# Attention of the first block: output products by query, reciprocals applied to a bank of four steps, differential maps kept as two heads

## The reference, cut to what matters

```python
a_out = neighbourhood_attention(na_q, na_k, na_v, na_rel_bias[l])               # 4 heads of 64, with a bias
a = softmax(s1) - lam * softmax(s2)                                              # differential: two maps, one v
b_out = einsum('bhqk,bhkd->bhqd', a, v)
b_out = rms_norm(b_out, diff_subln[l]) * (1.0 - lambda_init)                     # over the 64 of a head
c_out = gqa_attention(cq, ck, gq_v)                                              # 4 heads of 64
d_out = mla_attention(q_nope, q_rope, k_nope, k_rope, mla_v)                     # 4 heads, 96 wide in q and k
mix = concatenate([a_out, b_out, c_out, d_out]) @ w_o[l]                         # 256 features of each mixer
x = x + rms_norm(mix, post_mix_norm[l])
```

## Time and profile before

| | us |
|---|---|
| median of 3 runs | 1950.72 (1950.56 to 1950.94) |
| the profiled execution | 1953.09 |
| its span in the trace | 1951.3 |
| of it, `mixA` in layer 0 | 45.75, from 88.64 to 134.39 |
| of it, `mixA` in layer 1 | 45.75, from 433.17 to 478.92 |

### The profile page before, as it was taken

One profiled execution on the slowest core, in us unless ns is written; L12 is line 12 of the kernel. 1 busy time (PEld: TensorE's weight loads), 2 busy tenths in 40 slices (PEclk: granted clock), 3 DMA queues, 4 the chain that ended last, 5 costly groups with the idle time before them and its releaser, 6 DMA issues. The chain is left out here.

```text
span 1951.3 us, 29289 instructions
## 1 busy us (share of the span) xinstructions
PE 1876.3 (96%) x11654; PEld 1638.3 (84%) x11654; DVE 1134.9 (58%) x1643; ACT 923.8 (47%) x1271; POOL 176.5 (9%) x221
## 2 busy tenths in 40 slices
PE   7999999998999999899999999999899999999998
PEld 6668999766899978689998789998679998779997
DVE  6576555767655578554545465446765445775443
ACT  4564343556434446554435455345245435564342
POOL 1400000050000030001000001002501001000000
PEclk9999999999999999799999999999999999999999
DMA  7504555550355555126555425554825454525551
GB/s 249 182 23 131 182 193 186 182 173 17 124 194 193 192 187 176 55 87 216 173 202 185 173 87 176 199 185 164 226 90 173 172 195 151 198 103 173 185 202 66
DMA packets 185357, 313.10 MB, mean 160 GB/s; under 512 B 18877, under 2 KB 67571, under 8 KB 185267
## 3 DMA queue, kind: packets, MB, share of 16 engines
q1 hardware_dynamic: 182595, 304.24, 46.0%
q0 software_dynamic: 1376, 4.38, 0.9%
q10 hardware_dynamic: 1296, 3.24, 0.5%
HBM read 309.90 MB, written 1.94 MB: 160 GB/s over the span
## 5 line engine op out<-in xcount | busy, mean ns | idle before, releaser
L1468 DVE TENSOR_TENSOR w_lo<-raw,w_hi 128x2048 fp32r<-128x2048 f32 (+2 forms) x290 | 654.5, 2287 | 287.6 <-ACT w_hi L998 286.9
L998 ACT ACTIVATE w_hi<-raw 128x2048 fp32r<-128x2048 f32 (+2 forms) x290 | 533.3, 1877 | 105.4 <-PE tr L2039 59.8
L2037 PE MATMUL acc<-w_hi,hT_hi 128*128 128x512 f32 (+2 forms) x688 | 270.0, 392 | 15.5 <-DVE w_lo L1468 8.9
L2039 PE MATMUL acc<-w_hi,hT_lo 128*128 128x512 f32 (+2 forms) x688 | 266.4, 387 | 0.0
L2038 PE MATMUL acc<-w_lo,hT_hi 128*128 128x512 f32 (+2 forms) x688 | 266.2, 387 | 0.0
L2037 PE MATMUL acc<-w_hi,aux_hi 128*128 128x512 f32 x608 | 237.1, 390 | 0.0
L2038 PE MATMUL acc<-w_lo,aux_hi 128*128 128x512 f32 x608 | 237.1, 390 | 0.0
L2039 PE MATMUL acc<-w_hi,aux_lo 128*128 128x512 f32 x608 | 236.5, 389 | 0.0
L2037 PE MATMUL up<-hT_hi,w_hi 128*128 128x256 f32 x768 | 217.7, 283 | 0.6 <-DVE w_lo L1468 0.6
L2037 PE MATMUL tr<-hT_hi,w_hi 128*128 128x256 f32 x768 | 217.3, 283 | 0.0
L2038 PE MATMUL tr<-hT_lo,w_hi 128*128 128x256 f32 x768 | 217.3, 283 | 0.0
(11 more groups left out here) (365 smaller groups left out, 2774.8 us busy)
## 6 DMA issues: line engine op xcount, KB each, us to landing
raw<-in_mlp_w_up SPq DMA_DIRECT2D x64, 1024.0 KB, 6.5
raw<-in_mlp_w_down SPq DMA_DIRECT2D x64, 1024.0 KB, 5.5
raw<-in_ffn_w_gate_up SPq DMA_DIRECT2D x88, 512.0 KB, 4.8
raw<-in_ffn_w_down SPq DMA_DIRECT2D x22, 1024.0 KB, 5.0
raw<-in_w_in SPq DMA_DIRECT2D x16, 1024.0 KB, 8.2
raw<-in_sb_w_in SPq DMA_DIRECT2D x12, 1024.0 KB, 5.2
raw<-in_moba_w_in SPq DMA_DIRECT2D x12, 1024.0 KB, 5.1
raw<-in_nsa_w_in SPq DMA_DIRECT2D x10, 1024.0 KB, 5.7
```

The source lines that it names most:

```text
L998: nc.scalar.activation(w_hi[:, p0.slot, 0:p0.floats], raw[:, p0.slot, 0:p0.floats], ACT.Copy)\
L1468: nc.vector.tensor_tensor(w_lo[:, p0.slot, 0:m], raw[:, p0.slot, 0:m], f32(w_hi[:, p0.slot, 0:m]), ALU.subtract).then_inc(sem["lo_ready"], 1)
L2037: nc.tensor.matmul(dst, hi, whi, start=first, stop=False)
L2039: return nc.tensor.matmul(dst, lo, whi, start=False, stop=last)
```

## The change

1. `STEP_ORDER` becomes 8 differential, 4 gqa, 4 NA and 4 mla steps, so that each run of four steps fills one of two banks, `acc[:, j // 4 % 2, :]`: five groups of four steps.
2. All output products have the form of the differential ones: 128x128 of `probT` stationary, 64 columns of `v` moving, queries on partitions (4 products a step, one head after the other).
3. `pair_scaled` is gone. The row sums of a group are kept (`pair_den`); `group_rec` takes the 8 reciprocals of a group at once, `group_out` takes the whole bank out of PSUM times the reciprocals. For the two differential groups the second map's reciprocals are multiplied by -lambda first, and the two halves are added after. A differential step is now transposed with both its maps.
4. ACT copies the turned probabilities of even steps, DVE those of odd ones (`by_vector`), each in full width.
5. All outputs are turned back on PE, four transposes a group (`out_turn`), in turns 15, 17, 21 and behind the last output product; the group of tiles 2 and 3 goes through a bank of `tr`, the others through the bank of `acc` that held them. `out_hi` and `out_lo` write two tiles at once.

The diff, cut to its core:

```diff
-STEP_ORDER = (4, 12, 5, 13, 6, 7, 14, 8, 9, 15, 10, 11, 0, 1, 2, 3, 16, 17, 18, 19)
+STEP_ORDER = (4, 5, 6, 7, 8, 9, 10, 11, 12, 13, 14, 15, 0, 1, 2, 3, 16, 17, 18, 19)
-            g2.order = (4, 5, 2, 3, 0, 1, 6, 7)
+            g2.order = (2, 3, 4, 5, 0, 1, 6, 7)
 # ACT
-                                         accum_out=den[:, c:c + 1]).then_inc(sem["p_exp"], 1)
+                                         accum_out=den_at(i, u)).then_inc(sem["p_exp"], 1)
...
-                    if 0 <= i - TURN_LAG < len(steps):
+                    if 0 <= j < len(steps) and not by_vector(j):
...
+                    if i == 12:
+                        act.wait_ge(sem["o_taken"], n["o_taken"] + 2)
+                        nc.scalar.activation(group_cols(4), group_cols(1), ACT.Square).then_inc(sem["diff_sq"], 1)
+                    if i == 15:
+                        out_hi(1, tr[:, (turn_index(DIFF_TURN) - 1) % 2, :], 1)
+                    if i == 17:
+                        out_hi(2, acc[:, 0, :], 2)
+                    if i == 21:
+                        out_hi(3, acc[:, 1, :], 3)
+                out_hi(4, acc[:, 0, :], 4)
 # DVE
-            def pair_scaled(step, i):
...
+                def group_rec(g):
+                    dve.wait_ge(sem["p_exp"], n["p_exp"] + 8 * (g + 1))
+                    rec = pair_rec[:, 8 * (g % 2):8 * (g % 2) + 8]
+                    link(nc.vector.reciprocal(rec, pair_den[:, 8 * (g % 2):8 * (g % 2) + 8]))
+                    if g < 2:
+                        r1 = rec.rearrange("p (t a) -> p t a", t=TT)[:, :, 2:4]
+                        link(nc.vector.tensor_scalar(r1, r1, lam[:, 4:5], None, ALU.mult))
+                def group_out(g):
+                    dve.wait_ge(sem["o_done"], n["o_done"] + 4 * (g + 1))
...
+                    ins = nc.vector.tensor_tensor(dst.rearrange("p t (a c) -> p t a c", c=HD), group_bank(g), rec, ALU.mult)
+                    if g < 2:
+                        link(ins)
+                        ins = nc.vector.tensor_tensor(group_cols(1)[:, :, 128 * g:128 * g + 128], dst[:, :, 0:128],
+                                                      dst[:, :, 128:256], ALU.add)
+                    ins.then_inc(sem["o_taken"], 1)
...
+                    if 0 <= j < len(steps) and by_vector(j):
...
+                        nc.vector.tensor_copy(probT[:, j % 2, :], tr[:, turn_index(j) % 2, :]).then_inc(sem["pt_evac_d"], 1)
+                    if i in (4, 8, 12, 16, 20):
+                        group_rec(i // 4 - 1)
+                    if i in (8, 12, 16, 20):
+                        group_out(i // 4 - 2)
+                    if i == 13:
+                        diff_root()
+                    if i == 14:
+                        diff_gain()
+                    if i == 16:
+                        out_lo(1, tr[:, (turn_index(DIFF_TURN) - 1) % 2, :], 2)
+                    if i == 18:
+                        out_lo(2, acc[:, 0, :], 4)
+                    if i == 22:
+                        out_lo(3, acc[:, 1, :], 6)
+                group_out(4)
+                out_lo(4, acc[:, 0, :], 8)
 # PE
+                def out_turn(g, bank):
+                    at = group_cols(g)
                     for k in range(2):
                         for t in range(TT):
+                            last = nc.tensor.transpose(bank[:, S * k + P * t:S * k + P * t + P], at[:, t, P * k:P * k + P], ident)
                     last.then_inc(sem["hT_tr"], 1)
...
+                    if i == 15:
+                        turn_free(turn_index(DIFF_TURN) - 1)
+                        pe.wait_ge(sem["od_ready"], n["od_ready"] + 1)
+                        out_turn(1, tr[:, (turn_index(DIFF_TURN) - 1) % 2, :])
+                    if i == 17:
+                        pe.wait_ge(sem["o_taken"], n["o_taken"] + 3)
+                        out_turn(2, acc[:, 0, :])
+                    if i == 21:
+                        pe.wait_ge(sem["o_taken"], n["o_taken"] + 4)
+                        out_turn(3, acc[:, 1, :])
...
-                                last = nc.tensor.matmul(head["out"][:, P * step["qt"]:P * step["qt"] + P], head["v"][kt],
-                                                        probT[:, j % 2, at:at + P], start=kt == 0, stop=kt == TT - 1)
+                        for u in range(2):
+                            head = step["heads"][u]
+                            at = 256 * step["qt"] + HD * head["place"]
+                            for kt in range(TT):
+                                last = nc.tensor.matmul(acc[:, j // 4 % 2, at:at + HD],
+                                                        probT[:, j % 2, P * (TT * u + kt):P * (TT * u + kt) + P],
+                                                        head["v"][kt], start=kt == 0, stop=kt == TT - 1)
                         last.then_inc(sem["o_done"], 1)
+                pe.wait_ge(sem["o_taken"], n["o_taken"] + 5)
+                out_turn(4, acc[:, 0, :])
```

## The result

The changed kernel takes 1959.36 us (median of 4 runs, 1958.00 to 1960.29), the one before 1950.64 (4 runs, 1950.56 to 1950.94): 8.7 us more, a ratio of 1.0041, 95% interval 1.0028 to 1.0053. The profiled execution of the changed kernel took 1959.32, its span is 1957.5.

The account below looks back on a forecast made before the run. PE was taken to bound the kernel. Its work of 51.5 a stage, waits of 3.4 and slow clock of 1.2 replace 45.75: +10.3 a stage, +20.6 for two, giving 1971 us, range 1966 to 1977.

Parts of the forecast that it names:

- slow clock: A 1.2 GHz stretch on PE in each stage, behind the wait for `diff_gain`: +1.2 a stage after covering 0.5 of waits.
- I take 1.03, as the start-up of a group is paid once: PE's output groups of eight instructions: 0.59 + 4 x 0.11 = 1.03 each, +8.8 a stage.
- Transposes: 20 x 0.59: PE's transposes, four in every step at 0.59 a group: 11.8 a stage, which is +1.2.
- wait (a): PE in turn 15 waits for `diff_gain` ahead of the turning back: DVE's chain 8.9 against 7.2, wait 1.7.
- (b): PE's transposes of turn 17 wait for the bank of `tr`, through ACT's and DVE's halves: 0.4.
- (c): Last group: DVE must take the bank out before PE turns it, ahead of `w_o`: a wait of 0.9.
- some tenths: Copies of turned probabilities, late in turns where DVE also takes a bank out: in all 0.4 a stage.
- both are hidden, and nothing of their gain reaches the end: DVE's 2.1 and ACT's some 2.6 in two differential turns lie behind PE's 4.5, so their savings gain nothing.
- two signs of being wrong: The prediction is wrong if PE's waits in the stage exceed 6 us, or the eight instructions start closer than 0.1.
- Cheap streaming: Rival: the second head hides, output groups of 0.59, stage 49.6, +3.8 a stage, 1958; chance 0.06.
- DVE as the bound: Rival: copies or banks out of PSUM at 1.2 or more, 3 us more a stage, 1978 to 1982; chance 0.06.
- The faster case: Rival: output products cost only their columns, stage 44.3, median 1948; chance 0.03, of this 0.02 faster.

Follow-up runs that it names:

- same-half kernel: Kernel before, output products issued head by head and both heads of a pair written to the same 64 partitions: 1954.62 us, ratio 1.0020.
- the kernel with the late turning: Changed kernel with the last turning back moved behind the first 12 matmuls of the `w_o` product: 1960.25 us, ratio 1.0051.
- the new order alone: Kernel before with only the new `STEP_ORDER` and its bookkeeping; products, scaling, copies and norm in the old form: 1959.15 us, ratio 1.0045.
- the order with one filling: Kernel before in the new order, with the output products alone done twice in each differential step: 1954.93 us, ratio 1.0024.
- with both: Kernel before in the new order, with transposes and output products done twice in each differential step: 1955.46 us, ratio 1.0030.
- DVE's savings on top: Kernel before in the new order, sums of squares one turn later, and only the ratio of the two sums applied in differential steps: 1965.76 us, ratio 1.0071.

## Why the prediction was right and wrong

**Direction, and the mechanism of the outputs: right.** PE-bound turns, eight instructions per output group that have nothing to overlap with, 0.11 from one to the next: the changed kernel shows 0.84 to 1.04 a group, and the same-half kernel measured the overlap (0.60 against 1.02).

**Size: wrong.** The forecast had 56.1 a stage, the trace has 51.35: 9.5 of the 11.6 us by which the forecast of 1971 lay too high, for two stages. Term by term, in the forecast's own terms:

| term | forecast | measured |
|---|---|---|
| scores | 12.7 | 12.5 |
| transposes | 11.8 | 10.4 |
| outputs | 20.6 | 18.7 |
| late jobs | 4.0 | 3.6 |
| turning back | 2.4 | 1.7 |
| waits | 3.4 | 4.35 |
| slow clock | 1.2 | 0 |

(The measured ones are sums over PE's starts in layer 0, from a group's start to the next one's, without the waits.)

**The step that failed** is "I take 1.03, as the start-up of a group is paid once", and with it "Transposes: 20 x 0.59". These prices were read from starts in the kernel before, and they hold two things that come less often in the changed kernel: a change of the tile's shape behind the group, and a longer start of the group. Its transposes are at 0.49, or 0.44 in mla turns, and its outputs at 0.93, or 0.84 in mla turns, with 1.03 or 1.04 in only four groups. That is 1.9 (outputs) + 1.4 (transposes) + 0.7 (turning back) = 4.0 of the 4.75 by which the stage came out shorter. The last instruction of an output group in a differential and in an mla turn:

```profile
99.76 0.28 PE L2425 MATMUL acc<-proj,probT 128*128 128x64 f32 x1
...
127.71 0.28 PE L2425 MATMUL acc<-proj,probT 128*128 128x64 f32 x1
```

The next group starts 0.20 behind the first (99.96) and 0.11 behind the second (127.82). The first is followed by scores with a stationary tile of 64*128, the second by scores of 96*128. The single starts in both stages of the changed kernel, and in the kernel before outside its slow clock, all say the same. Behind the last instruction of outputs or of transposes, the next group of the stage starts 0.11 later at the least if its tile is 128*128 or 96*128 behind one of 128*128, and 0.20 later at the least if the tile changes to or from 128*64, or from 128*128 to 32*128 or 64*128. In the changed kernel nearly all that follow no wait are at these values. The price of 0.59 for four transposes came from 131.28, ahead of products of 128*64; in the changed kernel they stand ahead of 128*128. The forecast's own rows had the smaller value beside the larger: the transposes of the late jobs at 92.89, ahead of 128*128, took 0.49 up to 93.38, and I counted 0.59 for all.

A second 0.1 is at the start of an output group. From its first instruction to its second it takes 0.06 in 14 groups of the changed stage and 0.16 in 5, of which three stand behind the waits of 0.28, 0.36 and 0.60 (131.23: 0.94 instead of 0.84). In the kernel before it is 0.16 in seven of the eight differential groups. So the 0.59 of 104.47, and with it the 1.03, held that 0.1 as well; it is why an output group in a differential turn takes 0.93. That PE pays it where it comes to its input early is my reading of the three waits, and no run was made for it.

**The clock.** "With wait (a) of the same length I expect the same stretch behind it", +1.2. Both stages of the changed kernel have a granted clock of 1.00, although the wait of 1.50 ahead of line 2375 is there. It is not that such a wait never brings a fall: the kernel with the late turning has 10.2 us of slow clock behind the same wait in one of its stages, and the one with half of the products 6.8 and 3.4. What I missed is larger than 1.2, and didn't show in the total: the new order alone has 17 to 20 us of slow clock in a stage, most of it among the differential turns, and with the load of the new products that part is not there. The forecast had no term for the order, and that did no harm only because of the other part. The expectation for the order alone, by the same method, was 1948.5 to 1952, and the kernel took 1959.

**Waits.** (a) was 1.50 for 1.7, its chain on DVE from 109.60 to 118.22, 8.6 for 8.9. (b) was 0.82 for 0.4. (c) was 0.78 for 0.9. The forecast's "some tenths" of waits for copies were 1.24: 0.28, 0.36 and 0.60. The run with all copies on ACT says that the sharing out of the copies costs 2.3 a stage, 1.8 in waits. The forecast had two of these copies in its chain (a), at 1.3, and still wrote "both are hidden, and nothing of their gain reaches the end", from busy times alone. DVE was to be busy for well under 30 us and ACT for about 30; they are at 30.4 and 27.6. Neither of its two signs of being wrong came as it was meant: the waits are 4.35, under 6, and the eight instructions start 0.11 apart, all but the second, which mostly starts 0.06 behind the first.

**From the stage to the median.** 2 x 5.6 = 11.2 in the stages, 8.7 in the medians; the other 2.1 of the miss are here. The forecast took 2.4 off the profiled execution's time because the old one's lay so far above its median; the changed one's profiled execution lies at its median (1959.32 and 1959.36). That alone would have put the forecast 2.4 higher, so it doesn't explain the miss; it is of the size of what one execution's clock does elsewhere (the first stage began 2.4 earlier). A slip beside it: groups of 0.95 without the slow stretch give 1966, as the range has it, and not the 1967 among the rivals. Why the clock falls at other places in one execution than in another stays open, also why the order with one filling (stages of 50.4 and 51.0) has a median as low as with both (49.2 and 50.3).

**Rivals.** Cheap streaming would have given the nearest time, 1958, by groups of 0.59 that the trace doesn't have: a right number by a wrong reason. DVE as the bound is out, it is busy for 30.4 of 51.35. The faster case fell with the 0.11.

## What to carry to other kernels

A group's price from start to start depends on its neighbours. Take it from a place where the group behind it has the same tile shape as in the new kernel (0.11 or 0.20 behind the last instruction here), and where the engine comes as late to its input as it will there. If an engine of high share gets lighter work in a row, ask what its clock does: on TensorE, less work made stages longer here (51.8 with the order alone, 54.6 with DVE's savings on top), and repeating work made them shorter (49.2). And run the parts of a change apart before adding their prices: order and form cost 6.0 and 5.0 alone, and 5.6 together.

## What the hardware showed that I had not expected

- Eight instructions with 64 stationary columns each take 0.60 when the heads have different halves, whether they alternate or stand four by four, and 1.02 in the same half.
- A change of the stationary tile's shape between two groups goes with 0.09 more (0.20 instead of 0.11 from the last start to the next one): to or from 128*64, and from 128*128 to 32*128 or 64*128, but not from 128*128 to 96*128.
- In the kernel with the order alone TensorE fell to 1.2 GHz in a stretch with no idle time longer than 0.58 (it had waited 0.58, 0.28 and 0.51 in the ten us before), and stayed there for 17.1 us in which it was busy all the time. The ten us before:

```profile
88.00:98.00 10.00, 8.63 (x54) 5.99 (x52) 7.33 (x35) 6.70 (x24) 0.00 (x0) 1.00 0.01 2
```

  The Trainium skill, page "TensorE: Matmul & The Clock Gate", section "A second HAM failure mode: psum-queue depth-cycling", tells of a kernel whose short idle times between groups made the clock go up and down. The fall at 98.1 agrees with that in its short idle times; what followed is different, one long slow stretch without idle time and not an up and down.
- The same wait on the same instructions is followed by a slow stretch in one execution or stage and not in another (1.88 at 37.0 in the kernel before and the changed one; 1.5 at 118 with and without the late turning).
- At 1.2 GHz the scores take 1.16 instead of 0.63, but a pair of transposes only 0.48 instead of 0.27 to 0.37, and four output instructions 0.88 instead of 0.49 to 0.59.
